# Raw columns ahead of the norm's factors at four joints, and unread products in TensorE's waits

## The reference, cut to what matters

```python
def rmsnorm(x, g):
    y = xf * lax.rsqrt(jnp.mean(xf * xf, axis=-1, keepdims=True) + EPS)
    return (y * g).astype(x.dtype)

def step(S, inp):                       # 512 steps, two directions, 8 heads of 64
    sa = einsum('dbhvk,dbhk->dbhv', S, kk_t)
    S = S * w_t - sa * (kk_t * a_t) + v_t * k_t
    return S, einsum('dbhvk,dbhk->dbhv', S, r_t)

def conv_ffn(h, norm_g, w_up, conv_w, conv_b, w_down):
    u = dwconv_centred(rmsnorm(h, norm_g) @ w_up, conv_w, conv_b)   # 3 taps over tokens
    return (jax.nn.gelu(u[..., :D_FF]) * u[..., D_FF:]) @ w_down

def per_layer_embedding(h, p_i, norm_g, w_gate, w_proj):
    return jax.nn.sigmoid(rmsnorm(h, norm_g) @ w_gate) * (p_i @ w_proj)
```

## Time and profile before

| | |
|---|---|
| median of 3 runs (lowest, highest) | 3090.86 us (3089.98, 3091.36) |
| profiled execution, its time | 3095.25 us |
| profiled execution, its span, first to last instruction | 3093.5 us |
| mean granted clock of TensorE | 0.965 |
| TensorE, VectorE, ScalarE busy | 95%, 56%, 42% |
| instructions | 47616 |

### The profile page before, as it was taken

How to read it: one execution, slowest core, us unless ns; L and a number is a source line. 1 busy time by engine, 2 the same in 40 slices (tenths; PEclk the granted TensorE clock), 3 DMA queues, 4 the chain that set the end, 5 groups by cost and what they waited for, 6 DMA issues and landing times. The chain is left out here.

```text
span 3093.5 us, 47616 instructions
## 1 busy us (share of the span) xinstructions
PE 2946.8 (95%) x20174; PEld 2341.8 (76%) x20174; DVE 1717.9 (56%) x2344; ACT 1296.5 (42%) x2000; POOL 132.0 (4%) x222
## 2 busy tenths in 40 slices
PE   8998887899999999999999999999999999999999
PEld 6756776788887777788887786678888866678887
DVE  5355665477764685567674567553233577542333
ACT  4233332443334435543344446645243446553241
POOL 0400000000000000010000100100000101000000
PEclk9997887999999999999999999999999999999999
DMA  5210000456632222255652230023232310123222
GB/s 163 96 58 2 3 3 3 146 164 206 183 117 94 82 89 89 76 167 189 194 155 96 78 118 1 1 82 109 96 96 95 92 71 1 49 87 98 96 96 82
DMA packets 224019, 287.83 MB, mean 93 GB/s; under 512 B 8015, under 2 KB 163959, under 8 KB 217664
## 3 DMA queue, kind: packets, MB, share of 16 engines
q1 hardware_dynamic: 213488, 226.19, 23.4%
q0 software_dynamic: 8448, 54.34, 5.2%
q10 hardware_dynamic: 1872, 4.26, 0.4%
HBM read 280.57 MB, written 2.10 MB: 91 GB/s over the span
## 5 line engine op out<-in xcount | busy, mean ns | idle before, releaser
L232 DVE TENSOR_TENSOR weights_low_all<-weights,weights_high_all 128x2048 fp32r<-128x2048 f32 x195 | 446.7, 2291 | 483.4 <-ACT weights_high_all L226 475.5
L226 ACT CAST weights_high_all<-weights 128x2048 fp32r<-128x2048 f32 x195 | 372.4, 1910 | 544.3 <-PE ps L240 544.3
L238 PE MATMUL ps<-ffn_h_high,weights_high_all 128*128 128x512 f32 x704 | 275.7, 392 | 0.9 <-DVE weights_low_all L232 0.9
L239 PE MATMUL ps<-ffn_h_low,weights_high_all 128*128 128x512 f32 x704 | 274.4, 390 | 0.0
L240 PE MATMUL ps<-ffn_h_high,weights_low_all 128*128 128x512 f32 x704 | 274.4, 390 | 0.0
L238 PE MATMUL ps<-mlp_h_high,weights_high_all 128*128 128x512 f32 x512 | 200.9, 392 | 0.3 <-DVE weights_low_all L232 0.3
L239 PE MATMUL ps<-mlp_h_low,weights_high_all 128*128 128x512 f32 x512 | 199.7, 390 | 0.0
L240 PE MATMUL ps<-mlp_h_high,weights_low_all 128*128 128x512 f32 x512 | 199.6, 390 | 0.0
L238 PE MATMUL ps<-weights_high_all,mlp_hid_high 128*128 128x512 f32 x512 | 199.2, 389 | 0.0
L239 PE MATMUL ps<-weights_low_all,mlp_hid_high 128*128 128x512 f32 x512 | 199.2, 389 | 0.0
L240 PE MATMUL ps<-weights_high_all,mlp_hid_low 128*128 128x512 f32 x512 | 199.2, 389 | 0.0
(11 more groups left out here) (570 smaller groups left out, 6226.1 us busy)
## 6 DMA issues: line engine op xcount, KB each, us to landing
mod_w<-in_w_mod POOLq DMA_DIRECT2D x48, 1024.0 KB, 5.3
weights<-in_ffn_w_up SPq DMA_DIRECT2D x88, 512.0 KB, 5.7
weights<-in_w_mlp_in SPq DMA_DIRECT2D x32, 1024.0 KB, 5.4
weights<-in_w_mlp_out SPq DMA_DIRECT2D x32, 1024.0 KB, 5.1
weights<-in_ffn_w_down SPq DMA_DIRECT2D x24, 768.0 KB, 4.5
weights<-in_mix_w_in SPq DMA_DIRECT2D x13, 1024.0 KB, 5.3
weights<-in_na_w_qkv SPq DMA_DIRECT2D x12, 1024.0 KB, 5.2
weights<-in_w_in SPq DMA_DIRECT2D x12, 1024.0 KB, 5.4
```

Source lines behind the costliest of these rows:

```text
L226: nc.scalar.copy(st.high[s][:], st.raw[s][:]).then_inc(st.high_done, 1)
L232: nc.vector.tensor_tensor(st.low[s][:], st.raw[s][:], st.high[s][:], ALU.subtract).then_inc(st.split_done, 1)
L238: nc.tensor.matmul(out, lh, rh, start=start, stop=False)
L239: nc.tensor.matmul(out, lh, rl, start=False, stop=False)
```

## The change

Three things are changed together.

**1. `RawNorm` at four joints** ("mo" to feed-forward 0, "no" to feed-forward 1, and each feed-forward to its embedding). Unscaled residual tiles are turned and multiplied by the gain. Tiles 0 to 3 need only the first half of the columns and are turned inside the last group (output product) or last but one group (`Down`) of the stage before. The next stage's first group of products (`head_tensor`) stands in the same block, behind the last product. The row factor is applied later: for the feed-forward TensorE spreads it over all partitions (four fp32 products of ones with a diagonal), ScalarE copies it to `inverse`, and VectorE multiplies each sum by it into `z` before the taps; for the embedding it is the `scale` of the sigmoid. Weight splits in `ConvUp` go two groups ahead, and SP loads three. The output product's split input lies in the hidden tiles.

**2. `keep_running`**: products of the identity with a constant table into a free PSUM bank, which nothing reads. Eight stand behind the last product of "ao", of the last feed-forwards and of the embedding, five ahead of a `Norm`'s first transposes.

**3. The same in the recurrence**: two ahead of level_f's waits (levels 2 to 4), two in each level_x, two ahead of the fifth level, one behind each of seven chain steps.

```diff
+def keep_running(nc, cx, pe, bank, n):
+    for i in range(n):
+        nc.tensor.matmul(cx.ps[:, bank, i % 4 * P:(i % 4 + 1) * P], cx.ident[:], cx.blk64[:], start=True, stop=True)
+
+class RawNorm:
...
+    def turn(self, pe, k):
+        nc = self.nc
+        if k >= 4:
+            pe.wait_ge(self.low_done, k - 3)
+        pe.wait_ge(self.added, self.first + (1 + k // 4) * TT)
+        for t in range(TT):
+            mm = nc.tensor.transpose(self.bank(k)[:, t * P:(t + 1) * P], self.cx.x[:, t, k * P:(k + 1) * P], self.cx.ident[:])
+        mm.then_inc(self.turned, 1)
...
+    def head_vector(self, dve):
+        nc, cx = self.nc, self.cx
+        self.low(dve, 4)
+        dve.wait_ge(self.squared, 2 * TT)
+        nc.vector.tensor_tensor(self.inverse, cx.sums[:, 0, :], cx.sums[:, 1, :], ALU.add).then_inc(self.total, 1)
+        for k in range(5, KT):
+            self.low(dve, k)
+        dve.wait_ge(self.root, 1)
+        nc.vector.reciprocal(self.inverse, self.inverse).then_inc(self.inverted, 1)
...
 class Norm:
...
     def begin(self, pe):
+        if not self.weights:
+            keep_running(self.nc, self.cx, pe, 4, 5)
         for k in range(4):
             self.turn(pe, k)
...
 class ConvUp(Up):
...
-        pe.wait_ge(self.taps, g * 4 + 2 * j + 2)
+        pe.wait_ge(self.scaled, g * 2 + j + 1)
+
+    def head_tensor(self, pe):
+        nc, cx, norm = self.nc, self.cx, self.norm
+        pe.wait_ge(self.st.split_done, self.g0 + 1)
+        for k in range(KT):
+            norm.ready(pe, k)
+            if k == 0:
+                pe.wait_ge(norm.added, norm.first + TT + 2)
+            mm = [self.products(pe, 0, j, k) for j in range(2)]
+            if k == 0:
+                for n in range(4, KT):
+                    norm.turn(pe, n)
+        mm[0].then_inc(self.summed, 1)
+        mm[1].then_inc(self.st.used_up, 1)
+        pe.wait_ge(self.diagonal_done, TT)
+        for t in range(TT):
+            mm = nc.tensor.matmul(norm.bank(4)[:, t * P:(t + 1) * P], cx.ones[:], self.diagonal[:, t, :], start=True, stop=True)
+        mm.then_inc(self.spread, 1)
...
     def scalar(self, act):
...
         for g in range(self.n):
-            split_ahead(self.nc, self.st, act, self.g0 + g + 1, "high")
...
-                nc.scalar.activation(u[j][:], ps[:, self.bank(g, j), :], ACT.Identity, bias=self.column(f"b{l}", g, j),
+                nc.scalar.activation(u[j][:], self.z[j][:], ACT.Identity, bias=self.column(f"b{l}", g, j),
                                      scale=self.column(f"w{l}1", g, j)).then_inc(self.centre, 1)
+            split_ahead(nc, self.st, act, self.g0 + g + 2, "high")
             act.wait_ge(self.taps, g * 4 + 2)
             nc.scalar.activation(u[0][:], u[0][:], ACT.Gelu_apprx_tanh).then_inc(self.gelu, 1)
...
     def vector(self, dve):
...
             for j in range(2):
-                sums = ps[:, self.bank(g, j), :]
+                self.wait_sum(dve, g, j)
+                nc.vector.tensor_tensor(self.z[j][:], ps[:, self.bank(g, j), :], self.inverse[:], ALU.mult).then_inc(self.scaled, 1)
+            for j in range(2):
+                sums = self.z[j]
                 dve.wait_ge(self.centre, g * 2 + j + 1)
...
 class Down:
...
                     if q == self.nq - 1 and t < TT - 1:
                         mm.then_inc(self.summed, 1)
+                    if self.follow and g == self.n - 2 and t == 0:
+                        pe.wait_ge(self.modulation.read, self.modulation.l + 1)
+                        self.follow.norm.turn_first(pe)
...
             downs[1].tensor(pe, down_step(1))
+            if downs[1].follow:
+                downs[1].follow.head_tensor(pe)
+            elif downs[1].out is None:
+                pe.wait_ge(downs[1].added, TT + 1)
+                keep_running(nc, cx, pe, 4, 8)
...
+class EmbeddingHead:
...
+    def head_tensor(self, pe):
+        norm = self.norm
+        self.G.wait(pe, 0)
+        for t in range(TT):
+            pe.wait_ge(norm.added, norm.first + TT + t + 1)
+            for k in range(4):
+                if t == 0:
+                    norm.ready(pe, k)
+                mm = self.gate(0, t, k)
+            if t in (1, 2):
+                norm.turn(pe, 2 * t + 2)
+                norm.turn(pe, 2 * t + 3)
+        mm.then_inc(self.cx.stream.used_up, 1)
...
 def ple_phase(nc, cx, tag, head, p_in):
...
+                            if g == 1 and t == 2:
+                                turn_p()
+                                modulation.turn(pe, cx.ps[:, 6, :], columns_out)
...
+                pe.wait_ge(gate_done, TT + 1)
+                keep_running(nc, cx, pe, 0, 8)
...
-                        nc.scalar.activation(gate[:, t, :], cx.ps[:, t, :], ACT.Sigmoid).then_inc(gate_done, 1)
+                        nc.scalar.activation(gate[:, t, :], cx.ps[:, t, :], ACT.Sigmoid, scale=inverse[:, t:t + 1])\
+                            .then_inc(gate_done, 1)
...
             def level_f(lv):
+                if lv > 1:
+                    keep_running(nc, cx, pe, 4, 2)
...
             def level_x(lv):
+                if lv > 1:
+                    pe.wait_ge(sd.sem, sd.value(f"t{lv - 1}", m))
+                keep_running(nc, cx, pe, 5, 2)
                 pe.wait_ge(sd.sem, sd.value(f"fm{lv}", m))
...
+            keep_running(nc, cx, pe, 4, 2)
             pe.wait_ge(sa.sem, sa.value("x4", m))
...
                     mm.then_inc(sp_.sem, sp_.one(f"s{j}q{q}", m))
+                if j < NCH - 1:
+                    nc.tensor.matmul(ps[:, A2[0], 0:P], cx.ident[:], cx.blk64[:], start=True, stop=True)
```

More of the change, by code:

```diff
@@ L471, in token_groups, with add_product_phase @@
     return out
-def add_product_phase(nc, cx, tag, src, split, splits, gate=None, cold=False, x_from=None, squares=False):
+def add_product_phase(nc, cx, tag, G, src, split, splits, gate=None, cold=False, x_from=None, follow=None, junk=None):
     st = cx.stream
     NQ = len(splits)
-    G = Groups(cx, 2 * NQ)
     assert NQ % 2 == 0
+    junk = cx.ps[:, 7, :] if junk is None else junk
     with ExitStack() as ctx:
@@ L487, in add_product_phase @@
         cold_high, cold_low = (ctx.enter_context(nc.semaphore(f"{tag}_cold_{n}")) for n in ("high", "low"))
+        if follow:
+            follow.norm.behind(added, TT, squared)
         def quarter(parts, k):
@@ L495, in _ @@
                     gate.load(sp)
[L496 removed]
+                st.load(sp, G.g0 + G.n + (3 if follow else 2))
             @block.gpsimd
@@ L513, in _ @@
                             G.wait(pe, half * NQ + q)
+                        if follow and half and q == NQ - 1:
+                            follow.norm.turn_first(pe)
                         if half == 0 and q == 0:
@@ L898, with __init__ @@
 class Down:
-    def __init__(self, nc, cx, ctx, tag, up, splits, turn, gate=None, gated=None, squares=False, out=None, modulation=None, first=False):
+    def __init__(self, nc, cx, ctx, tag, up, splits, turn, gate=None, gated=None, squares=False, out=None, modulation=None, first=False,
+                 junk=None, follow=None):
         def sem(name):
@@ L911, in __init__ @@
             sem(n) for n in ("summed", "added", "scaled", "squared", "stored"))
+        if follow:
+            self.follow = follow()
+            self.follow.norm.behind(self.added, 0, self.squared)
     def bank(self, t):
@@ L954, in scalar @@
         for g in range(self.n):
-            split_ahead(nc, self.st, act, self.g0 + g + 1, "high")
+            if g or not self.up.two_ahead:
+                split_ahead(nc, self.st, act, self.g0 + g + 1, "high")
+            if self.follow and g == self.n - 2:
+                self.follow.norm.high_first(act)
             if self.squares and g == self.nq:
@@ L968, in vector @@
         for g in range(self.n):
-            split_ahead(nc, self.st, dve, self.g0 + g + 1, "low")
-            if self.modulation and not self.first and g == self.n - 2:
+            if g or not self.up.two_ahead:
+                split_ahead(nc, self.st, dve, self.g0 + g + 1, "low")
+            if self.modulation and not self.first and g == self.nq:
                 self.modulation.add(dve)
+            if self.follow and g == self.n - 2:
+                self.follow.norm.low_first(dve)
             if g % self.nq < self.nq - 1:
@@ L3538, in ple, with add_outputs @@
-        def ple(l):
-            with ExitStack() as hx:
-                h = parts(hx, f"ple_h{l}")
-                xn = hx.enter_context(nc.sbuf_tensor(f"ple_xn{l}", [P, TT, D], F32))
-                norm = Norm(nc, cx, hx, f"pn{l}", gain(f"ple_norm{l}"), h, [xn[:, t, :] for t in range(TT)], second=True)
-                ple_phase(nc, cx, f"ple{l}", norm, h, d["p"][l, 0])
+        def add_outputs(tag, o, gate=None, cold=False, x_from=None, follow=None, junk=None):
+            G = Groups(cx, 4)
+            add_product_phase(nc, cx, tag, G, cx.oT, o, (4, 4), gate, cold, x_from, follow and follow(), junk)
@@ L3566, in build_program @@
```

(3 more changed lines are left out.)

254 lines of the change are left out of this document (162 added, 92 removed).

## The result

The kernel after took **3055.02 us** (median of 4 runs, 3052.20 to 3059.25) against 3091.11 for the kernel before beside it: a ratio of 0.9882, 95% interval 0.9865 to 0.9899. Forecast were 3061 us, within 3044 to 3080. Measured once more in the last set of experiments, the same kernel took 3061.38 us beside 3094.22: 0.9896 (0.9880 to 0.9912).

What follows compares the result with a forecast made beforehand. TensorE, 95% busy, was taken as the bound. Gains of 21 (row factors), 4.5 (joints) and 4 us (recurrence) sum to 29.5, taking the span from 3093.5 to 3064 and the runs' median to 3061 us, range 3044 to 3080.

Steps and rivals of the forecast that it cites:

- the likeliest case's own range: Whole kernel: the forecast of 3061 us, chance 0.56, with its own range of 3051 to 3070 us.
- Row factors, 21 us: Four joints: row factor applied behind the products, so TensorE needn't wait for the normalization; 21 us gained, bounds 10 and 26.
- the four stretches: Two feed-forward to embedding joints, 6.3 us gained each; two products to feed-forward joints, 4.4 and 4.1 us.
- The row factor's price, 0: Up projection: 88 added VectorE products cost nothing; 10.8 us per summing group, VectorE deciding only above 11.5.
- The formula: Up projections: excess per group over TensorE's pace, times 8 summing groups, less 5 us lag, for each of four projections.
- the fourth rival: Up projections: VectorE becomes the bound at 13.5 us per group, 63 us lost, 3124 us; chance 0.03.
- Unread products at the joints, 4.5 us: Other joints: eight and five unread products fit the idle gap and remove half-clock stretches; 4.5 us gained, bounds -3 and 8.
- Unread products in the recurrence, 4 us: Recurrence: unread products keep the clock full in part; 4 us gained net, bounds 16 lost and 14 gained.
- half of 23 gained, minus 7.5 of cost: Recurrence: 23 us if the clock were never half, half taken as 11.5, minus 7.5 us for the unread products.
- The first (no rise of the clock, 3075 us): Recurrence: unread products don't raise the clock, 10 us lost instead of 4 gained, 3075 us; chance 0.17.
- The second (3050): Recurrence: clock held nearly throughout, 12 us gained, and the joints 7; 3050 us; chance 0.11.
- The third: Heads half exposed, or VectorE a little past 11.5 us per group: first part gives 10 us, 3072 us; chance 0.10.

## Why the prediction was right

The time lay within the likeliest case's own range, and the parts add up to it from about the right places.

- **Row factors, 21 us: held in the four stretches, too small in all.** The stretches give 19.6 (table above), each term near its forecast but "no", which lost 1.7 us to products at the half clock at 1246.5 us, where there had been none. The runs give more, 26 us (22 to 30). The half clock outside the recurrence shrinks too, from 95 us at 1.2 GHz to 62 in the kernel with the factors alone; the sum put that at nothing, and only the upper bound of 26 was placed for it ("clocks help"). Most of the 3 to 7 us by which the gain exceeds 29.5 lies here.
- **The row factor's price, 0: held, and its threshold too.** The forecast had 10.8 us per group and a decision above 11.5; VectorE needs 10.8, at 11.7 the loss is 12 us and at 13.2 it is 67. The formula (excess times 8, less 5 us of lag) gave 16 and 60, but for groups of 12.0 and 13.4 us. With the measured 11.73 and 13.18 it gives 7 and 53, so that it came so near was in part luck. It leaves out the products at the half clock behind the waits, with four more VectorE products some 17 us (ten times 1.5 to 1.9). That the debt is paid at the start of the down projection, where the fourth rival placed it inside the up projection, was not foreseen.
- **Unread products at the joints, 4.5 us: direction right, size off.** 2.6 to 3.1 us by the timelines, and about 1 to 6 by the runs (0.9915 to 0.9911 without the recurrence's, 0.9908 to 0.9889, the mean of the kernel after's two, with them).
- **Unread products in the recurrence, 4 us: within what the runs allow.** It was "half of 23 gained, minus 7.5 of cost". The half was low: time at 1.2 GHz between 250 us and the first product of "mo" was 93 to 123 us in the three profiles without them and 36 to 49 in the six with all of them, so about 60% went, not 50%. The cost was about right, 7 to 10 us for as many again. 14 minus 7 gives 7 us, as the stretches' means do; the medians give 2, 4.9 and 5 to 9, which doesn't rule out 4. The first profiled pair alone, 14.5, overstates it about twofold. That x1 to x4 had no wait to hide them was right, and the eight products there are what is lost.
- **The rivals.** The first (no rise of the clock, 3075 us) falls: with the products the two windows of the earlier trace rows show 0.93 to 0.98. It is what happens with products of 2 columns, 3078.9 us. The Trainium skill's rule against long idle gaps, from which it was drawn, doesn't decide here: dense products in waits of 0.8 us raised the clock, and thin ones in the same waits did not. The second (3050) lies at the edge of the first interval and outside the second, and its ground fails: 36 to 49 us were left at the half clock, and the joints gave less than 7. The third and the fourth (heads exposed, VectorE) fall with the timelines: no wait above 1.3 us between the last product of a stage and the second group of the next.

What stays open: why the same recurrence stretch takes 355 us in one execution and 363 in another of the same kernel. The time at 1.2 GHz is nearly the same (38 and 39 us); 2.7 us of the 7.6 stand as more idle time in which TensorE waits for nothing that the profile shows.

## What to carry to other kernels

Work that depends only on a row (a normalization's factor) can go behind the products if the engine that applies it has room; count that room in us per group, and remember that work done two groups ahead carries a few us of lag before it decides. Where TensorE falls to the half clock among short waits, fill the waits with dense unread products, and only the waits: where there is no wait, and beyond its length, each is cost. Judge such a change by several executions, since one profiled pair overstated this part about twofold.

## What the runs showed of the hardware

- An fp32 product of 2 columns takes as much of TensorE's stream as one of 128 (0.112 us from record to record at the full clock, 0.214 at the half, two records each), and 92 of them didn't keep the granted clock up (0.80 to 0.84 against 0.93 to 0.98).
- The clock was lost with TensorE 92% busy (64.5 of 70 us) and held with it 89% busy (62.3 of 70, the kernel with 60 products in the waits): busy time alone doesn't tell.
- A wait of about 2 us in a full stream can cost 1.5 to 1.9 us more, since eight or nine products behind it run at 1.2 GHz; with four more VectorE products this happened at ten places, and at others with the same wait it did not (660 to 700 us).
- Idle time that the profile puts down to nothing ("issue") varies much: between 252 and 520 us it is 3.0 us before, and 8.6 and 11.3 in two executions after. That filled waits bring it about isn't shown, since the two kernels with the row factors but without unread products in the recurrence have 6.0 and 6.4.

```profile
PE ps L1913 <- ACT rw_TH L2183: 4.0, 3, 1.6
...
PE ps L2021 <- issue: 2.5, 4, 1.1
PE ps L1957 <- issue: 2.3, 2, 1.2
```

These are the kernel after's waits of TensorE in the recurrence (us in total, times, longest). The 9.4 us for the levels' copies are gone from the list.
